# Turning 32 tiles of an expert table by VectorE in an earlier layer instead of by TensorE where they are used

## The chip, the cores and the metric

One core of one Trainium2 chip runs the whole program. The metric is the device time of one execution in microseconds. TensorE (PE) multiplies, VectorE (DVE) and ScalarE (ACT) do elementwise work, GpSimd (POOL) here does almost nothing but issue DMAs, SyncE (SP) issues the DMAs of the weight stream.

## What is computed

256 tokens of width 2048 pass through two blocks in float32. Only two parts matter here. The first is the feed-forward layer of the first block:

```python
def swiglu(h, w_gu, w_down):
    g, u = jnp.split(h @ w_gu, 2, axis=-1)
    return (jax.nn.silu(g) * u) @ w_down
```

with 5632 hidden units. The second is the last layer of the second block, which picks 128 of 16384 experts for each token (8 heads, 16 experts each), after q and the scores have been worked out:

```python
    def token_block(args):
        xb, eb, gb = args
        a = jnp.einsum('td,ted->te', xb, u_tab[eb])
        hidden = gb.astype(xb.dtype) * jax.nn.gelu(a)
        return jnp.einsum('te,ted->td', hidden, v_tab[eb])
```

An expert's number is `ia * 128 + ib`. `u_tab` and `v_tab` have 16384 rows of 2048 floats (8 KB), so that 128 rows with the same `ia` are a tile of 1 MB. A final norm follows. `setup_inputs()` fixes all values.

## The kernel before

**The weight stream.** All dense weights come as 292 tiles of 128x2048 floats through `ring` (4 slots), in halves called units. For each unit ACT writes a rounded leading part into `WH` (`split_hi`, L512 to L515), DVE the rest into `WL` (`split_lo`, L527 and L531), and PE multiplies three combinations of parts (L633). `WH` and `WL` hold 4 units, so ACT may begin a unit when PE has finished the one four before it. The first product of the feed-forward layer (`gu`) has 22 chunks of 8 units, the second (`down`) 44 tiles of 2 units, of which DVE handles the greater part in a loop of 4 rounds with 8 tiles (16 units) each.

**The expert stage** starts near 1820 us. Its order of work is a list written once, `ROW_ORDER`, of 576 entries that every engine walks. An entry is one transfer of 1 MB into one of 12 slots of `rows`. A "u" or "v" entry (256 of each) gathers for each of 128 tokens one row of the table by an indirect DMA from POOL; rows whose `ia` is below `N_DENSE` = 32 are skipped by the bounds check. For those 32 tiles the products are formed densely: a "turned" entry loads a whole tile of `u_tab`, a "dense" entry one of `v_tab`, both by plain DMAs from POOL (L1400). POOL issues entry n when entry n - 12 has been used, strictly in order.

- "u": DVE multiplies the gathered rows with the tokens and sums (L2566).
- "v": in the first part of the list by PE with a diagonal matrix that ACT writes (`DIAG`, L1873; 4 matmuls of 512 columns, L1313); after it mostly by DVE.
- "turned": PE turns the tile in four parts of four 128x128 transposes (`turn_u`, L1249) into a bank, ACT copies each part to `UT` (`keep_turned_u`, L1895), PE multiplies four of them at a time with the turned tokens `HNT` (`u_products`, L1260). Parts 0 and 1 are turned at the entry itself, parts 2 and 3 only in `finish_u`, which PE reaches at the next "v" or "turned" entry; POOL may refill the slot after part 3 has been turned (semaphore `raw_turned`).
- Each pair of tiles then passes through ACT and DVE for its gelu (`square_u`, `poly_u` L2609, `tanh_u`, `gelu_u`).

The 256 "u" entries form 16 groups of 16. `LEADS` says how many "v" entries are mixed into each group (119 in all), `U_TILES` how many "turned" ones (2 in groups 0 to 7, 4 in groups 8 to 11, none after). The other 137 "v" entries and the 32 "dense" ones follow. At the end of each group ACT waits for DVE's polynomial, takes its tanh (L1949), and only then goes on with diagonals. Matmuls in float32 show as two records each, so a "v" entry on PE shows as x8 and a tile's sixteen products as x32.

Of the kernel before, what the change touches and what calls it, by code (L numbers as in the profile page):

```python
# [9 lines left out]
P = 128  # L10
D = 2048
KD = D // P
TOK = 256
# [37 lines left out]
LEADS = [0] + [9] * 7 + [5] * 4 + [9] * 4  # L51
# [43 lines left out]
RAW_TURNED = 24  # L95
_count = {"dve": 0, "pe": 0, "turned": RAW_TURNED}
for _tab, _g, _j in ROW_ORDER:
    _by = "turned" if _tab == "turned" else "pe" if _tab == "dense" or _tab == "v" and by_matmul(PEER_K * _g + _j - N_LEAD) else "dve"
    _count[_by] += 4 if _by == "turned" else 1
    ROW_DONE.append((_by, _count[_by]))  # L100
FINISHED_AT = {}
for _n, (_tab, _g, _j) in enumerate(ROW_ORDER):
    if _tab == "turned":
        FINISHED_AT[_g] = next(n for n in range(_n + 1, ROW_LAST) if ROW_ORDER[n][0] in ("v", "turned"))
SQUARE_AT, POLY_AT, TANH_AT, GELU_AT = ({FINISHED_AT[2 * p + 1] + later: p for p in range(N_DENSE // 2)} for later in (2, 5, 8, 11))
# [9 lines left out]
WEIGH_AT.update({ROW_AT["u", 0, 3 + 2 * g]: g for g in range(EARLY)})  # L115
LAST_DENSE = ROW_AT["dense", N_DENSE - 1, 0]
# [114 lines left out]
def hybrid_block(nc, stream, par, consts, xT, memT, subk, gfin_row, u_tab, v_tab, bias_scratch, bias_rows, out):  # L231
# [5 lines left out]
    with ExitStack() as ctx:  # L237
# [27 lines left out]
        UT0, _ = place("UT0", [P, 4, P], at=at)  # L265
# [59 lines left out]
        AH, AL, _ = split_views("A", a - KD * TOK, 8)  # L325

# [85 lines left out]
        UT = [UT0[:, :, :], PA[:, W_GATE:W_GATE + 4 * P].rearrange("p (k i) -> p k i", i=P)]  # L412
# [5 lines left out]
        IA_GATE = [v.rearrange("p k i -> p (k i)").rearrange("p (k a) -> p k a", a=N_DENSE) for v in UT]  # L418
# [208 lines left out]
        def _(pe):  # L627
# [610 lines left out]
            def turn_u(n, d, part):  # L1238

                q = 4 * d + part  # L1240
                if part == 0:
                    pe.wait_ge(sem(f"row_in{n % ROWS}"), 16 * (n // ROWS + 1))
                if q >= 2:
                    pe.wait_ge(sem("transposes_kept"), TT + q - 1)
                else:
                    pe.wait_ge(sem("norm_leading"), 8 * len(TURNED) + 8)
                for k in range(4):
                    at = (4 * part + k) * P
                    last = nc.tensor.transpose(ps[:, 6 + q % 2, k * P:(k + 1) * P], rows[:, SLOTS[n % ROWS], at:at + P], ident)  # L1249
                last.then_inc(sem("raw_turned"), 1)  # L1250

            def u_products(d, part):

                q = 4 * d + part
                if d % 2 == 0 and part == 0 and d >= 4:
                    pe.wait_ge(sem("gelu_done"), 1 + d // 2 - 1)
                pe.wait_ge(sem("transposes_kept"), TT + q + 1)
                for k in range(4):
                    kt = 4 * part + k
                    last = mm(ps[:, 4 + d // 2 % 2, d % 2 * TOK:(d % 2 + 1) * TOK], UT[q % 2][:, k, :], HNT[kt // 8][:, kt % 8, :],  # L1260
                              start=kt == 0, stop=kt == KD - 1)
                last.then_inc(used, 1)

            def finish_u(n, d):

                u_products(d, 0)
                turn_u(n, d, 2)
                u_products(d, 1)
                turn_u(n, d, 3)
                u_products(d, 2)  # L1270
                u_products(d, 3)

            def turn_ids(tt):

                pe.wait_ge(sem("gates_ready"), 1 + PEER_H * (tt + 1))
                pe.wait_ge(sem("transposes_kept"), TT + 4 * N_DENSE)
# [18 lines left out]
            def dense_rows(n, c):  # L1295
                pe.wait_ge(sem(f"row_in{n % ROWS}"), 16 * (n // ROWS + 1))
# [7 lines left out]
            def gathered_rows(n, g, k):  # L1304
                pe.wait_ge(sem(f"row_in{n % ROWS}"), 16 * (n // ROWS + 1))
# [11 lines left out]
            k, turned = 0, None  # L1317
            for n, (tab, g, j) in enumerate(ROW_ORDER):
# [6 lines left out]
                elif tab == "turned":  # L1325
                    if turned:
                        finish_u(*turned)
                    turn_u(n, g, 0)
                    turn_u(n, g, 1)
                    turned = n, g  # L1330
                elif tab == "v" and (ROW_DONE[n][0] == "pe" or n >= FIRST_SHARED):
                    gathered_rows(n, g, k)
                    k += 1
                    if turned:
                        finish_u(*turned)
                        turned = None
# [3 lines left out]
        def _(pool):  # L1340
# [31 lines left out]
            pool.dma_start(bass.AP(bias_scratch.tensor, 0, [[KD, P], [1, KD]]), PA[:, W_GFFN:W_GFFN + KD]).then_inc(sem("bias_stored"), 16)  # L1372
            pool.wait_ge(sem("down_added"), 8)
# [12 lines left out]
            for n, (tab, g, j) in enumerate(ROW_ORDER):  # L1386
# [8 lines left out]
                elif n >= ROWS:  # L1395
                    by, count = ROW_DONE[n - ROWS]
                    pool.wait_ge(sem({"dve": "rows_dve", "pe": "rows_pe", "turned": "raw_turned"}[by]), count)
                if tab in ("dense", "turned"):
                    table, ia = (v_tab, g) if tab == "dense" else (u_tab, U_ORDER[g])
                    pool.dma_start(rows[:, SLOTS[n % ROWS], :], table[ia * PEER_KEYS:(ia + 1) * PEER_KEYS, :]).then_inc(sem(f"row_in{n % ROWS}"), 16)  # L1400
# [11 lines left out]
        def _(act):  # L1412
# [183 lines left out]
            W.until(T_IN2 - 2)  # L1596
# [1184 lines left out]
```

## Time and profile before

| | |
|---|---|
| median of 3 runs | 3148.67 us (3145.7 to 3165.38) |
| profiled execution | 3147.76 us, span 3146.0 us, mean granted clock 0.972 |
| PE busy | 2904.2 us (92%) |
| DVE busy | 2150.8 us (68%) |
| ACT busy | 1225.1 us (39%) |
| POOL busy | 974.6 us (31%) |
| DMA | 793.69 MB, mean 252 GB/s |

The span runs from the first to the last instruction; the execution's own time is 1.76 us longer. Busy shares are means over stages that differ: in the first 1820 us the weight stream sets the DMA traffic, after it the 1 MB entries of the expert stage. The granted clock is given as a share of full speed.

### The profile page before, as it was taken

How to read it: one execution, taken by the hardware profiler on the slowest of the kernel's cores; microseconds unless marked ns; L12 is line 12 of the kernel's file. 1: busy time of each engine (PE TensorE's matmuls, PEld its weight loads, DVE VectorE, ACT ScalarE, POOL GpSimd, SP SyncE). 2: the span in 40 equal slices, each digit the busy share in tenths (PEclk: the TensorE clock that was granted, in tenths of full speed). 3: DMA queues.
4: the chain of work that ended last, by engine and by line, in shares of the span. 5: the costliest groups of instructions: out<-in, count | busy, mean ns of one | idle time of the engine just before them, and what ended most of it. 6: DMA issues, size and time to landing. Idle time of an engine off the chain costs nothing.

```text
span 3146.0 us, 38089 instructions
## 1 busy us (share of the span) xinstructions
PE 2904.2 (92%) x13724; PEld 2187.2 (70%) x13724; DVE 2150.8 (68%) x2908; ACT 1225.1 (39%) x2125; POOL 974.6 (31%) x599
## 2 busy tenths in 40 slices
PE   9999999999999999999999949888888989978987
PEld 8888788888888889998888945554555655533333
DVE  5686665555565545465565887888887668887777
ACT  5555555555553345355655521111111235700000
POOL 0011000000000000000000056777764678886774
PEclk9999999999999999999999979999998999999998
DMA  7444545555555555543443468999997899999997
GB/s 272 146 165 145 185 182 190 188 187 187 188 185 187 187 187 181 189 157 137 153 177 143 182 262 322 366 380 377 370 365 294 321 338 366 360 389 389 387 405 300
DMA packets 128209, 793.69 MB, mean 252 GB/s; under 512 B 30982, under 2 KB 30998, under 8 KB 32670
## 3 DMA queue, kind: packets, MB, share of 16 engines
q0 software_dynamic: 84000, 475.94, 39.2%
q1 hardware_dynamic: 43920, 313.73, 27.4%
q8 instruction: 90, 1.47, 0.2%
q10 hardware_dynamic: 144, 2.10, 0.2%
q14 instruction: 55, 0.45, 0.0%
HBM read 925.55 MB, written 4.22 MB: 296 GB/s over the span
## 4 chain that ended last, share of the span: by engine, by line
PE 69%; POOL 9%; DVE 8%; DMA 8%; issue 3%; ACT 3%; DVEq 0%; ACTq 0%; SPq 0%; POOLq 0%
PE ps L633 48%; POOL rows L1405 9%; PE ps L1313 6%; PE ps L1260 4%; DMA rows<-peer_v 4%; DMA rows<-peer_v,arena 3%; PE ps L1300 3%; DVE arena L2566 3%; PE ps L1249 1%; PE ps L741 1%; DVE WL L531 1%; ACT arena L1885 0%; PE ps L941 0%; PE ps L1291 0%; DMA rows<-peer_u,arena 0%
## 5 line engine op out<-in xcount | busy, mean ns | idle before, releaser
L531 DVE SCALAR_TENSOR_TENSOR WL<-ring,PA,WH 128x512 fp32r<-128x512 f32 x896 | 633.2, 753 | 459.5 <-ACT WH L515 442.6
L1313 PE MATMUL ps<-rows,rstd 128*128 128x512 f32 x1108 | 531.9, 632 | 158.1 <-ACT rstd L1873 103.4
L2566 DVE CUSTOM_DVE_ANT_0 arena<-rows,arena 128x2048 f32<-128x2048 f32 x256 | 586.9, 2292 | 64.5 <-DMA rows<-peer_u,arena 25.8
L514 ACT ACTIVATE WH<-ring,PA 128x512 fp32r<-128x512 f32 x448 | 324.1, 723 | 545.8 <-PE ps L633 398.4
L1405 POOL DMA_INDIRECT rows<-peer_u,arena x256 | 456.2, 1782 | 213.5 <-DVE WL L531 85.1
L1313 PEld LDWEIGHTS ps<-rows,rstd 128*128 128x128 f32 x1108 | 217.8, 202 | 428.6 <-issue 366.6
L1405 POOL DMA_INDIRECT rows<-peer_v,arena x256 | 447.0, 1746 | 171.5 <-issue 65.5
L633 PE MATMUL ps<-WH,HH 128*128 128x512 f32 x1120 | 442.3, 395 | 4.2 <-DVE WL L531 4.2
L633 PE MATMUL ps<-WH,HL 128*128 128x512 f32 x1120 | 437.7, 391 | 0.0
L633 PE MATMUL ps<-WL,HH 128*128 128x512 f32 x1120 | 437.2, 390 | 0.0
L2570 DVE SCALAR_TENSOR_TENSOR XR<-rows,arena,XR 128x2048 f32<-128x2048 f32 (+1 forms) x119 | 276.7, 2325 | 79.9 <-DMA rows<-peer_v,arena 71.3
L515 ACT ACTIVATE WH<-ring,PA 128x512 fp32r<-128x512 f32 x448 | 317.1, 708 | 0.0
L633 PE MATMUL ps<-HH,WH 128*128 128x256 f32 x1088 | 309.5, 284 | 4.7 <-DVE WL L531 3.2
L633 PE MATMUL ps<-HL,WH 128*128 128x256 f32 x1088 | 307.8, 283 | 0.0
L633 PE MATMUL ps<-HH,WL 128*128 128x256 f32 x1088 | 307.8, 283 | 0.0
L1377 POOL DMA_DIRECT2D arena<-bias_rows x2 | 1.8, 908 | 904.0 <-DVE XR L2275 904.0
L1300 PE MATMUL ps<-rows,arena 128*128 128x512 f32 x512 | 236.8, 618 | 37.7 <-DMA rows<-peer_v 37.7
L527 DVE TENSOR_TENSOR WL<-ring,WH 128x1024 fp32r<-128x1024 f32 x128 | 156.0, 1224 | 164.5 <-ACT WH L512 163.8
L633 PEld LDWEIGHTS ps<-WH,HH 128*128 128x128 f32 x1120 | 211.2, 189 | 49.1 <-DVE WL L531 5.7
L633 PEld LDWEIGHTS ps<-WH,HL 128*128 128x128 f32 x1120 | 210.8, 188 | 44.5
L633 PEld LDWEIGHTS ps<-WL,HH 128*128 128x128 f32 x1120 | 211.3, 189 | 43.1 <-issue 0.5
L1300 PEld LDWEIGHTS ps<-rows,arena 128*128 128x128 f32 x512 | 99.7, 198 | 173.0 <-issue 119.2
(391 smaller groups left out, 4186.6 us busy)
## 6 DMA issues: line engine op xcount, KB each, us to landing
ring<-stream SPq DMA_DIRECT2D x292, 1024.0 KB, 4.8
rows<-peer_u POOLq DMA_DIRECT2D x32, 1024.0 KB
rows<-peer_v POOLq DMA_DIRECT2D x32, 1024.0 KB
rows<-peer_u,arena POOLq DMA_INDIRECT x256
rows<-peer_v,arena POOLq DMA_INDIRECT x256
arena<-xT SPq DMA_DIRECT2D x4, 512.0 KB, 8.8
bias_rows<-bias_scratch POOLq DMA_DIRECT2D x1, 2048.0 KB, 11.4
arena<-xT ACTq DMA_DIRECT2D x1, 2048.0 KB, 10.7
```

What stands on the lines that cost most here:

```text
L514: nc.scalar.activation(half_tile(WH, u)[:, 0:CH], raw_half(u)[:, 0:CH], ACT.Copy, scale=gain[0])
L515: nc.scalar.activation(half_tile(WH, u)[:, CH:UNIT], raw_half(u)[:, CH:UNIT], ACT.Copy, scale=gain[1]).then_inc(hi_done, 1)
L527: nc.vector.tensor_tensor(half_tile(WL, u), raw_half(u), half_tile(WH, u).bitcast(f32), ALU.subtract).then_inc(split, 1)
L531: ins = nc.vector.scalar_tensor_tensor(out=half_tile(WL, u)[:, s], in0=raw_half(u)[:, s], scalar=gain[d], in1=half_tile(WH, u).bitcast(f32 ...
L633: last = mm(o, l, r, start=start and n == 0, stop=stop and n == 2)
L741: last = mm(o, k[:, 2 * h + d, tk * P:(tk + 1) * P], q[:, 2 * h + d, tq * P:(tq + 1) * P], start=d == 0, stop=d == 1)
L1260: last = mm(ps[:, 4 + d // 2 % 2, d % 2 * TOK:(d % 2 + 1) * TOK], UT[q % 2][:, k, :], HNT[kt // 8][:, kt % 8, :], start=kt == 0, stop=kt = ...
L1300: last = mm(ps[:, 4 * tt + q, :], DENSE[c][:, tt * P:(tt + 1) * P], rows[:, SLOTS[n % ROWS], q * CH:(q + 1) * CH], start=False, stop=tt == ...
L1313: last = mm(ps[:, 4 * tt + q, :], DIAG[:, k % DIAGS, :], rows[:, SLOTS[n % ROWS], q * CH:(q + 1) * CH], start=n == mine[0], stop=n == ends[q])
L1405: nc.gpsimd.indirect_dma_start(out=rows[:, SLOTS[n % ROWS], :], out_offset=None, in_=u_tab if tab == "u" else v_tab, in_offset=bass.Indire ...
L2566: ins = V.tensor_tensor_reduce(out=JUNK, in0=rows[:, SLOTS[n % ROWS], :], in1=HN[:, tt, :], scale=1.0, scalar=0.0, op0=ALU.mult, op1=ALU.a ...
L2570: ins = V.scalar_tensor_tensor(out=XN[:, tt, s], in0=rows[:, SLOTS[n % ROWS], s], scalar=GA[:, tt, at:at + 1], in1=XN[:, tt, s], op0=ALU.m ...
```

## The change

The 32 tiles of `u_tab` are turned ahead of time and stored. From the start of the feed-forward layer on, POOL loads each tile as four DMAs of 256 KB (pieces of 2 KB: 32 rows by a quarter of the columns on 32 partitions each) into two half buffers, DVE turns the 32x32 blocks of each half with one instruction (`turn_tile`, 1024 elements per partition), and POOL stores the 1 MB result to a DRAM table `u_turned`, waits until it has landed, and loads the next tile. Twenty tiles are turned in `gu`, one a chunk, after unit 3; the other twelve in `down`, three a round, after units 1, 6 and 11 of 16. The expert stage then loads tiles from `u_turned` and PE multiplies them at once (`turned_rows`); its transposes, ACT's copies and their waits are removed. The columns of the tokens are picked with a step of 16 to match. "v" entries move: groups 8 to 11 get 8 in place of 5, groups 12 to 14 get 8 in place of 9, so that 128 stand in the first part and 128 after it. ACT waits once, ahead of the next norm, until all tiles are stored. The gelu steps of a pair stand 4, 7, 10 and 13 entries after its second tile (before: 2, 5, 8, 11 after the entry that finished it).

```diff
-LEADS = [0] + [9] * 7 + [5] * 4 + [9] * 4
+LEADS = [0] + [9] * 7 + [8] * 7 + [9]
...
+LANDED = [32 * N_DENSE, 32 * N_DENSE, 16 * N_DENSE] + [0] * (ROWS - 3)
...
+        U_TURNED, a = take(a, KD, 4, 32)
+        U_HALF0, _ = take(a, 2, 512)
+        U_HALF = [U_HALF0, rstd[:, :, :].rearrange("p (b x) t -> p b (x t)", b=2)]
+        u_turned = nc.dram_tensor("u_turned", (N_DENSE, P, D), f32, kind="Internal").ap()
...
-                        last = nc.tensor.transpose(ps[:, b, k * TOK + tt * P:k * TOK + (tt + 1) * P], HN[:, tt, (2 * b + k) * P:(2 * b + k + 1) * P], ident)
+                        last = nc.tensor.transpose(ps[:, b, k * TOK + tt * P:k * TOK + (tt + 1) * P], HN[:, tt, 2 * b + k:D:KD], ident)
...
+            def turned_rows(n, d):
+
+                pe.wait_ge(sem(f"row_in{n % ROWS}"), LANDED[n % ROWS] + 16 * (n // ROWS + 1))
+                if d == 0:
                     pe.wait_ge(sem("norm_leading"), 8 * len(TURNED) + 8)
...
+                if d % 2 == 0 and d >= 4:
                     pe.wait_ge(sem("gelu_done"), 1 + d // 2 - 1)
...
+                u = rows[:, SLOTS[n % ROWS], :].rearrange("p (k i) -> p k i", i=P)
+                for k in range(KD):
+                    last = mm(ps[:, 4 + d // 2 % 2, d % 2 * TOK:(d % 2 + 1) * TOK], u[:, k, :], HNT[k // 8][:, k % 8, :],
+                              start=k == 0, stop=k == KD - 1)
+                last.then_inc(sem("rows_pe"), 1)
...
+            pool.wait_ge(sem("small_weights"), 4)
+            for d in range(N_DENSE + 1):
+                if d:
+                    pool.wait_ge(sem("small_weights"), 4 + 2 * d)
+                    pool.dma_start(u_turned[d - 1], U_TURNED.rearrange("p k b i -> p (k b i)")).then_inc(sem("row_in2"), 16)
+                    pool.wait_ge(sem("row_in2"), 16 * d)
+                if d < N_DENSE:
+                    for b in range(4):
+                        at = (U_ORDER[d] * PEER_KEYS + 32 * b) * D
+                        pool.dma_start(U_HALF[b // 2][:, b % 2, :], bass.AP(u_tab.tensor, at, [[512, 4], [D, 32], [1, 512]])).then_inc(sem(f"row_in{b // 2}"), 16)
             pool.wait_ge(sem("down_added"), 8)
...
+                    tile = v_tab[g * PEER_KEYS:(g + 1) * PEER_KEYS, :] if tab == "dense" else u_turned[g]
+                    pool.dma_start(rows[:, SLOTS[n % ROWS], :], tile).then_inc(sem(f"row_in{n % ROWS}"), 16)
...
             W.until(T_IN2 - 2)
+            act.wait_ge(sem("row_in2"), LANDED[2])
...
+            def turn_tile(d, i=0, per=0):
+
+                for h in range(2):
+                    dve.wait_ge(sem(f"row_in{h}"), i * (32 * per) + 32 * (d + 1))
+                    V.transpose(U_TURNED[:, :, 2 * h:2 * h + 2, :],
+                                U_HALF[h].rearrange("p b (d k) -> p k b d", k=KD)).then_inc(sem("small_weights"), 1)
...
                 for m in range(first, 8):
                     split_lo(dve, 2 * (T_GU + 4 * n) + UNITS + m, i)
+                    if 1 <= n < N_GU - 1 and m == 3:
+                        turn_tile(n - 1, i, 2)
...
+                    for m in range(8):
+                        split_lo(dve, 2 * (T_DOWN + 4 * j) + UNITS + m, i)
+                        if (j, m) in ((0, 1), (0, 6), (1, 3)):
+                            turn_tile(N_GU - 2 + 2 * j + m // 6, i, 3)
                     act_batch(j + 2, i)
```

## Rows read from the trace of the kernel before

**Rows 1.** Part 2 of the page, 40 slices: DMA busy share in tenths
```profile
DMA  7444545555555555543443468999997899999997
```

**Rows 2.** Part 4 of the page: the chain that ended last, by line
```profile
PE ps L633 48%; POOL rows L1405 9%; PE ps L1313 6%; PE ps L1260 4%; DMA rows<-peer_v 4%; DMA rows<-peer_v,arena 3%; PE ps L1300 3%; DVE arena L2566 3%; PE ps L1249 1%; PE ps L741 1%; DVE WL L531 1%; ACT arena L1885 0%; PE ps L941 0%; PE ps L1291 0%; DMA rows<-peer_u,arena 0%
```

**Rows 3.** Stretches: busy PE, PEld, DVE, ACT, POOL; granted clock; DMA share; GB/s
```profile
600.00:900.00 300.00, 300.00 (x1352) 248.31 (x1351) 173.31 (x258) 160.22 (x258) 0.00 (x0) 1.00 0.52 189
950.00:1150.00 200.00, 200.00 (x859) 161.15 (x858) 102.93 (x90) 76.27 (x72) 0.00 (x0) 1.00 0.53 189
1850.00:1900.00 50.00, 15.66 (x56) 10.72 (x56) 41.83 (x72) 3.73 (x9) 19.40 (x12) 0.60 0.47 169
1900.00:2300.00 400.00, 350.50 (x1147) 203.74 (x1148) 344.19 (x614) 60.26 (x155) 314.44 (x185) 0.96 0.97 373
2300.00:2750.00 450.00, 390.33 (x1655) 259.95 (x1654) 350.32 (x475) 172.45 (x422) 313.55 (x191) 0.96 0.90 339
2350.00:2450.00 100.00, 78.54 (x324) 55.29 (x323) 71.11 (x131) 18.76 (x41) 50.42 (x37) 0.90 0.76 283
2750.00:3100.00 350.00, 300.23 (x707) 132.03 (x706) 273.49 (x135) 8.90 (x24) 254.64 (x167) 0.95 0.99 392
```

**Rows 4.** Timeline of PE from 2368 us: start, length, line, operation
```profile
2368.84 1.89 PE L1260 MATMUL ps<-arena,UT 128*128 128x256 f32 x8
2370.57 0.60 PE L1249 MATMUL ps<-CO,rows 128*128 128x128 f32 x4
2371.01 1.89 PE L1260 MATMUL ps<-arena,PA 128*128 128x256 f32 x8
...
2376.63 1.04 PE L1249 MATMUL ps<-CO,rows 128*128 128x128 f32 x8
2378.83 3.67 PE L1313 MATMUL ps<-rows,rstd 128*128 128x512 f32 x8 [1.17 <-ACT rstd L1873]
```

**Rows 5.** Timeline of POOL: two issues that waited
```profile
1896.36 0.99 POOL L1405 DMA_INDIRECT rows<-peer_v,arena  x1 [19.46 <-PE ps L1249]
...
2373.64 0.57 POOL L1400 DMA_DIRECT2D rows<-peer_u  x1 [15.73 <-PE ps L1249]
```

**Rows 6.** Waits from 2300 to 2750 us: total, times, longest
```profile
DVE arena L2609 <- ACT arena L1908: 56.4, 9, 8.6
PE ps L1313 <- ACT rstd L1873: 55.9, 24, 7.7
...
POOL rows L1400 <- PE ps L1249: 47.0, 6, 15.7
```

**Rows 7.** Groups by line, 1850 to 3146 us: busy, mean ns, idle before
```profile
L2566 DVE CUSTOM_DVE_ANT_0 arena<-rows,arena 128x2048 f32<-128x2048 f32 x249 | 570.8, 2292 | 63.3 <-DMA rows<-peer_u,arena 25.8 <-DVE arena L2545 3.4 <-DVE arena L2603 3.1
...
L1249 PE MATMUL ps<-CO,rows 128*128 128x128 f32 x496 | 70.3, 275 | 4.0 <-DMA rows<-peer_u 4.0
```

**Rows 8.** VectorE, 950 to 1150 us by form, and line 2297 by itself
```profile
L527 DVE TENSOR_TENSOR WL<-ring,WH 128x1024 fp32r<-128x1024 f32 x72 | 88.2, 1225 | 97.4 <-ACT WH L512 97.4
...
L2252 DVE TENSOR_SCALAR A_h<-arena 128x1024 fp32r x8 | 5.5, 689 | 0.0
...
L2297 DVE TENSOR_TENSOR arena<-arena,PA x8: 566/570/596, 1287.3 to 1290.7; 128x240 f32<-128x240 f32 x8
```

**Rows 9.** Timeline of ACT, `down`: two units, seven apart
```profile
949.87 1.06 ACT L512 ACTIVATE WH<-ring 128x1024 fp32r<-128x1024 f32 x1 [1.74 <-PE ps L633]
...
969.47 1.06 ACT L512 ACTIVATE WH<-ring 128x1024 fp32r<-128x1024 f32 x1 [1.74 <-PE ps L633]
```

**Rows 10.** DMA issues: count, KB each, median us to landing
```profile
ring<-stream SPq DMA_DIRECT2D x292, 1024.0 KB, 4.8
...
arena<-memT POOLq DMA_DIRECT2D x1, 2048.0 KB, 9.0
...
arena<-subkeys POOLq DMA_DIRECT2D x1, 1024.0 KB, 7.7
...
out<-arena SPq DMA_DIRECT2D x1, 1024.0 KB, 3.9
```

More of the change, by code:

```diff
@@ L94 @@
 ROW_DONE = []
-RAW_TURNED = 24
-_count = {"dve": 0, "pe": 0, "turned": RAW_TURNED}
+_count = {"dve": 0, "pe": 0}
 for _tab, _g, _j in ROW_ORDER:
-    _by = "turned" if _tab == "turned" else "pe" if _tab == "dense" or _tab == "v" and by_matmul(PEER_K * _g + _j - N_LEAD) else "dve"
-    _count[_by] += 4 if _by == "turned" else 1
+    _by = "pe" if _tab in ("dense", "turned") or _tab == "v" and by_matmul(PEER_K * _g + _j - N_LEAD) else "dve"
+    _count[_by] += 1
     ROW_DONE.append((_by, _count[_by]))
[L101 to L105, printed above, removed]
+SQUARE_AT, POLY_AT, TANH_AT, GELU_AT = ({ROW_AT["turned", 2 * p + 1, 0] + later: p for p in range(N_DENSE // 2)} for later in (4, 7, 10, 13))
 BATCH_AT = {}
@@ L1315, in gathered_rows @@
                 last.then_inc(sem("rows_pe"), 1)
-            k, turned = 0, None
+            k = 0
             for n, (tab, g, j) in enumerate(ROW_ORDER):
@@ L1325, in _ @@
                 elif tab == "turned":
[L1326 to L1330, printed above, removed]
+                    turned_rows(n, g)
                 elif tab == "v" and (ROW_DONE[n][0] == "pe" or n >= FIRST_SHARED):
@@ L1881, in one_hots @@
                 else:
-                    act.wait_ge(used, 2 * N_TILES + 4 * N_DENSE)
+                    act.wait_ge(sem("rows_pe"), ROW_DONE[ROW_AT["turned", N_DENSE - 1, 0]][1])
                 v = ONE_HOT[n % 2]
@@ L1901, in square_u @@
             def square_u(p):
-                act.wait_ge(used, 2 * N_TILES + 8 * p + 8)
+                act.wait_ge(sem("rows_pe"), ROW_DONE[ROW_AT["turned", 2 * p + 1, 0]][1])
                 if U_ORDER[2 * p] // 8 in (2, 3):
@@ L1920, in _ @@
             DIAG_READ = [ROW_DONE[n][1] for n, row in enumerate(ROW_ORDER) if row[0] == "v" and ROW_DONE[n][0] == "pe"]
-            k, turned = 0, None
+            k = 0
             for g in range(EARLY):
@@ L1932, in _ @@
                     tanh_u(TANH_AT[n])
-                if tab == "turned":
-                    if turned is not None:
-                        keep_turned_u(turned, 2)
-                        keep_turned_u(turned, 3)
-                    keep_turned_u(g, 0)
-                    keep_turned_u(g, 1)
-                    turned = g
                 if tab == "v" and (ROW_DONE[n][0] == "pe" or n >= FIRST_SHARED):
@@ L1942, in _ @@
                     k += 1
-                    if turned is not None:
-                        keep_turned_u(turned, 2)
-                        keep_turned_u(turned, 3)
-                        turned = None
                 if tab == "u" and j == PEER_K - 1:
```

56 lines of the change are left out of this document (6 added, 50 removed).

## The prediction, made before the changed kernel was run

> **What bounds the kernel now.** I read the slices first: DMA is about half busy for the first 23 slices and nearly full after that, with a dip near slice 30 [rows 1]. The chain that ended last puts 48% of the span on L633, the matmuls of the weight stream; the rest is a mix of POOL's issues, DMA landings, PE and DVE [rows 2]. So there are two programs in a row, and the stretches price them. In the feed-forward layer PE is busy all the time at full clock while DVE has 173.31 of 300 us of work and the DMA engines are 0.52 busy: PE is the bound, and DVE, POOL and DMA have room [rows 3]. In the expert stage the DMA engines are 0.97 busy from 1900 to 2300 us and 0.99 from 2750 to 3100 us, at 373 and 392 GB/s: there DMA is the bound, though PE has 350.5 of 400 us and DVE 344.2. Two stretches fall out: 1850 to 1900 us (share 0.47) and 2300 to 2750 us (0.90, and 0.76 in its worst 100 us) [rows 3]. What the change can win lies in these two holes; it does not touch the bytes that the stage moves. Rows of POOL name the reason for both: it stood 19.46 us in the first and 15.73 us in the second until PE had turned a tile (L1249), because entries are issued in order and a "turned" slot comes free only after its last transposes [rows 5].
>
> **What leaves PE.** On PE's timeline a step of eight product records takes 1.73 us (2368.84 to 2370.57) and a group of four transposes 0.44 us (to 2371.01) [rows 4]. A tile has four of each: 6.9 + 1.8 = 8.7 us, and 6.9 us after the change. 32 x 1.8 = 56 us of PE leave. None of that is gain where DMA bounds; it counts through the holes. ACT's copies go too, and with them the 1.17 us by which a "v" entry waited for a diagonal queued behind a copy [rows 4], part of 55.9 us of such waits from 2300 to 2750 us [rows 6]. The 7.7 us ones among them stay possible: ACT still waits for DVE at a group's end.
>
> *First hole.* The slot of the second tile now comes free when its products are done and no longer waits for the first "v" entry, which itself waits for ACT and DVE. Up to 19 us of issue come forward. But DVE is busy 41.8 of these 50 us, the same share as later (344.2 of 400), and at most 12 entries can be held ahead, so not all is kept: between 0 and -19 us, I take -12.
>
> *1900 to 2300 us.* DMA share 0.97; smaller waits on PE go. 0 to -8 us (to the 0.99 of the later stretch, 400 x 0.02), I take -4.
>
> *Second hole.* At a share of 0.97 the same transfers take 450 x 0.90 / 0.97 = 417.5 us, -32.5; by the rate 450 x 339 / 373 = 409 us, -41. I take -34, nearer the share, as a byte costs the same in both. What is late next is PE: a group of groups 8 to 11 now holds 4 tiles (27.7 us) and 8 "v" entries of about 3.5 us (28.1), 55.8 us. Its DMA work: 24 gathered entries of which a quarter of the rows is skipped (32 of 128 `ia`), and 4 whole ones, 22 MB of 1.049e6 bytes each at 373 GB/s, 61.9 us. PE would be 0.90 busy. From 1900 to 2300 us it was 0.88 busy beside a DMA share of 0.97, so it nearly fits; for the last 2% and engines waiting in order I add 5 us. From 0 to -41, taken -29.
>
> *Moved "v" entries.* Nine of the tail's 137 come forward, 9 x 0.75 x 1.049 = 7.1 MB, moved at 373 instead of 392 GB/s: +1 us. Eight DVE steps of 2.29 us [rows 7] in the tail become PE steps of 3.5 us, both beside a full DMA.
>
> *Tokens with a step of 16.* 32 transposes of 0.11 us each on an otherwise waiting path, at most doubled: 0 to 3.5 us, I take +1. Loads from the new table have the same 8 KB rows: nothing.
>
> **What is added in the feed-forward layer.** The trace has no block transpose. Contiguous two-input work costs 1225 ns for 1024 elements and 2292 ns for 2048 [rows 7, 8], so 1.04 ns an element and 0.16 us fixed. The nearest row is L2297, which also reads every 16th element: 570 ns for 240, so 1.71 ns an element [rows 8]. For 1024: T = 1.9 us. Bounds: 0.69 us (L2252, one input) and 2.45 us (twice L527). I take 1.9, as the access is the same; a pair costs 3.8 us, 32 pairs 122 us of DVE. In `gu` a chunk takes 22.2 us (100 PE records of the 1352 in 300 us), DVE is busy 12.8 us of it. The pair delays what is queued behind it on DVE, units 4 and on, for which PE waits. Its cover is the lead of three units (8.3 us) less ACT's and DVE's work on one, (173.31 + 160.22)/300 x 2.77 = 3.1 us: 5.2 us, more than 3.8. Cost nothing; without the cover up to 20 x 3.8 = 76 us.
>
> The Trainium skill, page "SBUF — State Buffer", section "Specifications (TRN2)", says that an access needs at least two hits in a 16-byte line for full bandwidth. By it a read with a step of 64 bytes is slow; the row of L2297 agrees, and with full speed instead (1.2 us each) nothing in the sum would change.
>
> The chain tile by tile is store, landing, four loads, landing, transposes; DVE waits for the loads with the stream's units behind it, and PE behind those. Landing of the store: between 3.9 us (1 MB out, alone on SP's queue) and 7.7 us (`subkeys`, POOL), I take 5.5. Loads: between 4.8 us (`ring`, 1 MB) and 9.0 us (`memT`, 2 MB), I take 6.5, as four issues follow each other [rows 10]. Transposes that are not hidden: when DVE waits, the first half is turned while the second lands, 2.8 us. Handing over 0.3 us. C = 15.1 us; from 9.7 us (3.9 + 4.8 + 0.7 + 0.3) to 22 us (7.7 + 9.0 + 4.9 + 0.3). In `gu` there are 22.2 us for it: hidden. In `down` a unit takes 19.6 / 7 = 2.80 us [rows 9], and from the first of the twelve tiles to the last are 58 units, 162.4 us, for 11 C; DVE's lead there is 3 x 2.80 - 1.06 - 1.23 = 6.1 us [rows 8, 9]. So the stall is 11 C - 168.5 where that is positive: 11 x 15.1 = 166, nothing, but the threshold of C = 15.3 is close. I take +2. ACT's new wait comes after the last store by more than four tiles of the stream: nothing. SP's ring loads share the engines: 2.1 MB more in 14.9 us is 141 GB/s, by the 0.53 for 189 GB/s a share of 0.92 in all [rows 3]; with four slots of 5.6 us ahead they have cover. POOL's next queued work, the bias loads, waits for the layer's end anyway.
>
> Against the four small loads stands the Trainium skill, page "DMA: Bandwidth & Descriptors", section "Bandwidth": batch to 1 MiB or more; it gives 6.15 us for a 1 MB load from GpSimd. As an estimate from that page, two such transfers make C 15.4 us and the stall 1 us; no row here shows a 256 KB piece.
>
> **Sum.** -12 - 4 - 29 + 1 + 1 + 2 = -41 us against the profiled execution's 3147.76 us: 3107 us. That execution lies 0.9 us under the median of 3148.67 us, which is the figure to compare with.
>
> **Rivals.**
> *The chain doesn't fit `down`.* One mechanism: C above 15.3 us, while DVE holds back the stream. For it: loads, stores and stream share engines at 0.92, and a landing under load may be far above the 4.8 us of a half-busy stretch; against it, 2 MB landed in 9.0 us. At C = 20: 51.5 us of stall, -43 + 51.5, so 3156 us. It is slower than before from C = 19.2 on. Chance 0.13.
> *PE or the coupling of engines stays the bound in groups 8 to 11.* In the worst 100 us PE was only 0.79 busy though it was the one waited for [rows 3]. DVE's 56.4 us for ACT's squares and the group-end waits speak for it [rows 6]; that these waits came from late transposes (POOL's 47.0 us) against. At 0.79 a group takes 55.8 / 0.79 = 70.6 us, 35 us more in four groups than DMA needs; the second hole stays open: -12 + 1 + 1 + 2, 3140 us. Chance 0.17.
> *DMA runs everywhere as in the tail.* -19 - 8 - 41 + 1, 3081 us. For it the rate of 392 GB/s; against it PE's and DVE's loads of near 0.9. Chance 0.13.
> The forecast, 3090 to 3125 us, has 0.57.
>
> **Range and chances.** 3082 to 3152 us: it leaves out half of the third rival and most of the first. Within 1% (31.5 us, about what a measurement of this kernel can tell from no change) lie a fifth of the forecast's cases, the second rival and most of the first: 0.37. Faster by more (under 3117 us): 0.58. Slower by more needs C above 22 us: 0.05.
>
> **What would show it.** In `gu`: PE busy throughout, transposes of about 1.9 us. In `down`: twelve tiles 14 to 17 us apart and PE still full; waits of DVE on U's loads with PE behind them would be the first rival. At 1850 to 1900 us a DMA share near 0.7 and no wait of POOL near 19 us. From 2300 on a share of 0.95 or more, groups 8 to 11 about 62 us each, L1895 gone; many waits of POOL for L1260's successor there would be the second rival. The tail shorter by 18 us. I would be wrong most likely through C, which rests on landings under a load that the trace doesn't show.

## The result, and the profile after

The changed kernel takes 3209.98 us (median of 4 runs, 3200.68 to 3217.28) against 3149.43 us for the kernel before (median of 4): ratio 1.0185, interval 1.0146 to 1.0225. It is 61 us slower; the forecast was 41 us faster, with a range of 3082 to 3152 us. The profiled execution took 3217.28 us, with a span of 3215.5 us.

The slices of the page show where. These three are the granted clock, the DMA share and the count of packets of the changed kernel:

```profile
PEclk9999999999999888999999998989999999999999
DMA  7344558999997786544444447999999999999997
...
DMA packets 167628, 860.93 MB, mean 268 GB/s; under 512 B 58118, under 2 KB 58134, under 8 KB 67998
```

Against [rows 1] two things changed. The dip near slice 30 is gone: the expert stage is full from end to end. And ten slices of the feed-forward layer, half busy before, now stand at six to nine tenths, while the clock dips at their end: PE stood there for part of the time. The chain that ended last says nothing of the layer: its shares add up to 60%, and the list in order of time begins at 1311 us, behind the layer. So its 14% for the stream's products must not be set against the 48% of [rows 2].

```profile
PE 29%; POOL 10%; DVE 8%; DMA 8%; issue 3%; ACT 2%; DVEq 0%; ACTq 0%; POOLq 0%
PE ps L632 14%; POOL rows L1384 10%; PE ps L1289 6%; DVE arena L2538 3%; DMA rows<-peer_v 3%; PE ps L1276 3%; PE ps L1246 3%; DMA rows<-peer_u,arena 2%; DMA rows<-peer_v,arena 2%; PE ps L940 0%; DVE WL L530 0%; PE ps L996 0%; PE ps L1267 0%; ACT arena L1865 0%; DVE arena L223 0%
```

Lengths of the stages, each between the starts or ends of fixed instructions (VectorE's last work on the small weights just ahead of `gu`, the first split of the layer's activations, the first addition of `down`'s sums, the first "u" entry, a group's last tanh, the last sum). They are worked out from the traces, in microseconds:

| kernel | `gu` | `down` | to the first "u" | 16 groups | tail |
|---|---|---|---|---|---|
| before | 456.3 | 259.1 | 648.2 | 949.1 | 365.0 |
| after | 483.3 | 350.6 | 649.4 | 917.0 | 344.9 |
| change | +27.0 | +91.5 | +1.2 | -32.1 | -20.1 |

So the stage that the change is made for gained 52 us, more than the 43 us of the sum, and the layer that was to hide the turning lost 118.5 us. The changes add up to 67.5 us, and with 2.0 us ahead of the layer to the 69.5 us between the two profiled executions. The medians are 61 us apart, as the profiled execution was the slowest of the four.

Two stretches of the layer, of the changed kernel (columns as in [rows 3]):

```profile
600.00:900.00 300.00, 291.31 (x1296) 238.69 (x1295) 211.40 (x273) 153.67 (x246) 42.74 (x65) 0.99 0.94 271
950.00:1150.00 200.00, 154.89 (x614) 121.87 (x613) 99.91 (x83) 56.43 (x57) 26.31 (x40) 0.90 0.76 215
```

PE issued 1296 records in 300 us of `gu` in place of 1352, and 614 in 200 us of `down` in place of 859. In `down` it is busy for 154.89 of 200 us. The stream and the turning together moved only 215 GB/s there, so the bytes are not what fills the time.

What everyone waited for in `down`, from 925 to 1260 us (total, times, longest):

```profile
POOL u_turned L1346 <- DVE arena L2183: 222.8, 13, 33.0
ACT WH L511 <- PE ps L632: 218.8, 75, 14.4
DVE arena L2183 <- DMA arena<-peer_u: 108.7, 12, 13.9
PEld ps L632 <- DVE WL L526: 72.8, 12, 11.0
PE ps L632 <- DVE WL L526: 67.6, 11, 10.6
POOL arena L1351 <- DMA u_turned<-arena: 52.0, 12, 4.7
```

Read from the third row: DVE waited 108.7 us for the tiles' loads, about once a tile; PE waited behind it for DVE's part of the stream (67.6 us, 11 times); ACT waited behind PE. One link of it, on POOL's timeline (start, length, line, operation, idle before):

```profile
999.29 0.58 POOL L1346 DMA_DIRECT2D u_turned<-arena  x1 [13.36 <-DVE arena L2183]
1004.48 1.37 POOL L1351 DMA_DIRECT2D arena<-peer_u  x2 [4.61 <-DMA u_turned<-arena]
1005.84 1.35 POOL L1351 DMA_DIRECT2D rstd<-peer_u  x2
1024.34 0.58 POOL L1346 DMA_DIRECT2D u_turned<-arena  x1 [17.15 <-DVE arena L2183]
```

and on DVE's:

```profile
1004.16 2.36 DVE L526 TENSOR_TENSOR WL<-ring,WH 128x1024 fp32r<-128x1024 f32 x2
1020.38 1.89 DVE L2183 STREAM_TRANSPOSE arena<-arena 128x1024 f32<-128x1024 f32 x1 [13.86 <-DMA arena<-peer_u]
1022.20 1.85 DVE L2183 STREAM_TRANSPOSE arena<-rstd 128x1024 f32<-128x1024 f32 x1
1023.97 4.59 DVE L526 TENSOR_TENSOR WL<-ring,WH 128x1024 fp32r<-128x1024 f32 x4
```

This round of the chain took 25.05 us: 5.2 us from the store's issue to the first load's, 15.9 us until DVE had the first half, 3.7 us of transposes, 0.3 us to the next store. DVE stood for 13.86 us of it; once released it did four units in a row, the ones that PE was waiting for. The twelve stores of the tiles turned in `down`, from 978.45 to 1232.77 us, are 23.1 us apart on average, and the twenty of `gu`, from 486.23 to 937.66 us, 23.8 us. C is not 15.1 us. On average over eleven rounds of `down` the four parts were 4.9, 13.6, 4.3 and 0.3 us, and DVE stood waiting for the loads in all eleven, so that the chain and not the stream set these intervals. (The expectations below speak of 23.5 and, for eight loads, of 19.6 us: these are means over fewer of the tiles. From here on C is the mean of the eleven intervals of the last twelve stores.)

The DMA issues (count, KB each, median us to landing) name the part that is long:

```profile
u_turned<-arena POOLq DMA_DIRECT2D x32, 1024.0 KB, 4.4
...
arena<-peer_u POOLq DMA_DIRECT2D x64, 256.0 KB, 8.3
rstd<-peer_u POOLq DMA_DIRECT2D x64, 256.0 KB, 12.7
```

The store lands in 4.4 us. The loads of the first half take 8.3 us and those of the second 12.7 us, where a load of 1 MB of `ring`, issued by SP, takes 5.1 us. A DMA of a quarter of the size takes about twice as long.

### The profile page after: what moved, and what is told of

The parts are those of the page before. It is cut to its first block, busy times and chain, and to the rows that moved or that the text cites. A ratio compares the mean times of both kernels' runs of the same rounds, so it can differ in the third digit from the quotient of the medians.

```text
span 3215.5 us, 37171 instructions
## 1 busy us (share of the span) xinstructions
PE 2907.2 (90%) x13276; PEld 2165.1 (67%) x13276; DVE 2243.8 (70%) x2964; ACT 1159.6 (36%) x2005; POOL 1104.7 (34%) x759
## 2 busy tenths in 40 slices
DMA packets 167628, 860.93 MB, mean 268 GB/s; under 512 B 58118, under 2 KB 58134, under 8 KB 67998
## 4 chain that ended last, share of the span: by engine, by line
PE 29%; POOL 10%; DVE 8%; DMA 8%; issue 3%; ACT 2%; DVEq 0%; ACTq 0%; POOLq 0%
PE ps L632 14%; POOL rows L1384 10%; PE ps L1289 6%; DVE arena L2538 3%; DMA rows<-peer_v 3%; PE ps L1276 3%; PE ps L1246 3%; DMA rows<-peer_u,arena 2%; DMA rows<-peer_v,arena 2%; PE ps L940 0%; DVE WL L530 0%; PE ps L996 0%; PE ps L1267 0%; ACT arena L1865 0%; DVE arena L223 0%
## 5 line engine op out<-in xcount | busy, mean ns | idle before, releaser
L1289 PE MATMUL ps<-rows,rstd 128*128 128x512 f32 x1172 | 560.6, 631 | 147.7 <-ACT rstd L1853 90.6
L1289 PEld LDWEIGHTS ps<-rows,rstd 128*128 128x128 f32 x1172 | 231.3, 202 | 443.9 <-issue 359.5
L1384 POOL DMA_INDIRECT rows<-peer_v,arena x256 | 471.1, 1840 | 125.9 <-issue 67.0
L2542 DVE SCALAR_TENSOR_TENSOR XR<-rows,arena,XR 128x2048 f32<-128x2048 f32 (+1 forms) x111 | 257.9, 2324 | 77.6 <-DMA rows<-peer_v,arena 69.7
L1246 PE MATMUL ps<-arena,rows 128*128 128x256 f32 x1024 | 228.0, 381 | 7.7 <-DMA rows<-u_turned 6.6
L511 ACT ACTIVATE WH<-ring 128x1024 fp32r<-128x1024 f32 x128 | 134.6, 1058 | 265.8 <-PE ps L632 258.8
L1246 PEld LDWEIGHTS ps<-arena,rows 128*128 128x128 f32 x1024 | 195.5, 191 | 48.1 <-issue 15.9
## 6 DMA issues: line engine op xcount, KB each, us to landing
rstd<-peer_u POOLq DMA_DIRECT2D x64, 256.0 KB, 12.7
rows<-peer_v,arena POOLq DMA_INDIRECT x256, 13.6
```

Source lines behind the costliest of these rows:

```text
L511: nc.scalar.activation(half_tile(WH, u), raw_half(u), ACT.Copy).then_inc(hi_done, 1)
L1289: last = mm(ps[:, 4 * tt + q, :], DIAG[:, k % DIAGS, :], rows[:, SLOTS[n % ROWS], q * CH:(q + 1) * CH], start=n == mine[0], stop=n == ends[q])
L1384: nc.gpsimd.indirect_dma_start(out=rows[:, SLOTS[n % ROWS], :], out_offset=None, in_=u_tab if tab == "u" else v_tab, in_offset=bass.Indire ...
L2542: ins = V.scalar_tensor_tensor(out=XN[:, tt, s], in0=rows[:, SLOTS[n % ROWS], s], scalar=GA[:, tt, at:at + 1], in1=XN[:, tt, s], op0=ALU.m ...
```

## The experiments

The kernel before took 3152.5, 3153.66 and 3153.28 us on the chips of the three sets of runs below; ratios are against it.

### The two halves of the change, each alone

The stage without the turning (e1):

```diff
-            for d in range(N_DENSE + 1):
-                ... (stores and loads of POOL)
-                        turn_tile(n - 1, i, 2)
-                            turn_tile(N_GU - 2 + 2 * j + m // 6, i, 3)
-                    tile = ... else u_turned[g]
+                    tile = ... else u_tab[U_ORDER[g] * PEER_KEYS:(U_ORDER[g] + 1) * PEER_KEYS, :]
```

> The changed kernel without its work in the feed-forward layer: no loads, transposes or stores there; the expert stage loads the unturned tiles of the table from u_tab in their place (same shape, same bytes; the values of these 32 tiles' products are wrong). If the two parts add up, the expert stage keeps what the two traces show: its first u row to its last sum took 3136.9 - 1822.8 = 1314.1 us before and 3206.4 - 1944.5 = 1261.9 us after, 52 us less, so 3149 - 52 = 3097 us. A rival: part of the 52 us comes from elsewhere (the table in internal DRAM, the state in which the stage begins); then the time is above 3110 us.

Measured: 3102.85 us, ratio 0.9841 (0.981 to 0.9872). `gu` 456.3, `down` 260.6, groups 918.3, tail 347.4 us. The time lies between the 3097 us expected and the 3110 us of the rival.

The turning without the stage (e2, the kernel before, with POOL's loop and `turn_tile`, and its own expert stage):

```diff
+            for d in range(N_DENSE + 1):
+                ... (stores and loads of POOL, as in the change)
+                        turn_tile(n - 1, i, 2)
+                            turn_tile(N_GU - 2 + 2 * j + m // 6, i, 3)
```

> The kernel before, with the changed kernel's loads, block transposes and stores added in the feed-forward layer and their result not used. If the loss lies only in that layer and does not depend on the new expert stage: 3148 + 121 = 3269 us, with the twelve tiles of the second product about 24 us apart. If the loss came from something else that changed with the stage, it stays well under 3240 us.

Measured: 3264.95 us in one run. `gu` 484.2, `down` 353.3, groups 944.9, tail 361.7 us; the last twelve stores are 23.4 us apart. It is 4 us from the 3269 us expected.

The halves add up: the stage alone gains some 50 us, the turning alone costs about 112 us, together about the 60 us lost. The whole loss is made in the layer, and the gain in the stage does not depend on it. Removing the stores and loads together with the transposes does not yet say which of them costs.

### Which property of the loads is slow

The four loads of a tile read pieces of 2 KB with the pattern `[[512, 4], [D, 32], [1, 512]]`: the outermost dimension is the 4 strips of columns. The next kernels keep the number of loads and their bytes and change the pattern alone, or the size of the piece.

Rows outermost, 128 of them (e3):

```diff
-  at = (U_ORDER[d] * PEER_KEYS + 32 * b) * D
-  bass.AP(u_tab.tensor, at, [[512, 4], [D, 32], [1, 512]])
+  at = U_ORDER[d] * PEER_KEYS * D + 512 * b
+  bass.AP(u_tab.tensor, at, [[D, 128], [1, 512]])
```

> The changed kernel with each of the four loads of a tile taking a piece of 2 KB from each of 128 rows of the tile, one row for each partition, in place of four strips of 32 rows (same bytes, same size of piece, same number of DMAs; the columns land in other places, so the 32 tiles' products are wrong). Theory A, the order of the strips (slowest dimension of 4) makes the loads slow: they land in 7 us or less instead of 8 to 13, the tiles of the second product come 15 to 18 us apart and the time falls by 60 us or more, to 3150 us or less. Theory B, pieces of 2 KB are slow by themselves, or the weight stream's bursts hold the loads back: no change, 3200 to 3217 us.

Measured: 3124.18 us in one run; `gu` 456.4, `down` 285.2 us; 17.2 us a tile. Theory A holds. The trace of this run gives no landings; from a tile's first load to DVE's first transpose passed 7.0 us on average in `down`, in place of 13.6.

Two loads of 512 KB, 4 KB a row (e4):

```diff
+  bass.AP(u_tab.tensor, at, [[D, 128], [512, 2], [1, 512]])     # two of these in place of four
```

> The changed kernel with two loads of 512 KB for a tile, 4 KB from each row, one row for each partition (same bytes; the 32 tiles' products are wrong). If the size of the piece or the number of DMAs is what makes the loads slow, they land in about 6 us, the chain falls to 16 to 18 us and the time to 3120 to 3150 us, while the kernel with 2 KB from each row stays slow. If the weight stream's bursts hold any load back, it stays within 20 us of the changed kernel, 3195 us or more.

Measured: 3106.84 us in one run; `gu` 456.3, `down` 267.9 us; 15.8 us a tile. It is 13 us below the expected range, and as e3 was not slow, the size of the piece or the number of DMAs is not what makes the changed kernel's loads slow.

With the same bytes in the same number of loads as the changed kernel, the rows-outermost form takes 5.9 us less a tile, and `gu` loses nothing. But it differs in two ways: the 4 is gone, and a load takes 2 KB of each of 128 rows in place of the whole of 32. So the outermost dimension was changed by itself, with the rows-outermost form as the base:

```diff
+  [[D, 4], [4 * D, 32], [1, 512]]       # e6
+  [[D, 16], [16 * D, 8], [1, 512]]      # e7
```

> As the kernel with one row for each partition (3124 us), with the same 128 pieces of 2 KB in each load, but dealt to the partitions by a pattern that counts 4 outermost: partition 32c + r takes row c + 4r. The 32 tiles' products are wrong. Theory A1, the slowest dimension of 4 is what makes the loads slow (few DMA engines share the work): back to 3195 to 3217 us, small packets back to some 58 thousand. Theory A2, it was the addresses (four neighbouring pieces of one row in four strips): stays at 3115 to 3135 us.

> The same with 16 outermost: partition 8c + r takes row c + 16r. The 32 tiles' products are wrong. By theory A1 16 is enough for all engines: 3115 to 3135 us. If any pattern that is not a plain run of rows is slow: 3195 us or more.

Measured, one run each: 3231.01 us with 4 outermost (`gu` 496.8, `down` 350.8 us, 23.2 us a tile) and 3135.51 us with 16 (`gu` 456.4, `down` 292.5 us, 18.1 us a tile). The first is 14 us above the range of theory A1 and the second at its upper end. The page's count of packets, first of the kernel with 4 outermost, then of that with 16:

```profile
DMA packets 167628, 860.93 MB, mean 267 GB/s; under 512 B 58118, under 2 KB 58134, under 8 KB 67998
```

```profile
DMA packets 143053, 860.73 MB, mean 275 GB/s; under 512 B 33543, under 2 KB 33559, under 8 KB 43423
```

and their stretch from 950 to 1150 us, in the same order:

```profile
950.00:1150.00 200.00, 160.37 (x635) 126.62 (x633) 104.76 (x93) 60.36 (x65) 26.39 (x40) 0.90 0.78 216
```

```profile
950.00:1150.00 200.00, 178.36 (x716) 140.84 (x714) 123.19 (x95) 63.74 (x61) 29.59 (x56) 0.94 0.79 268
```

Both read rows, 2 KB of each, into 128 partitions, four loads a tile. The one with 4 outermost is the changed kernel over again: the same 58118 small packets, 216 GB/s at a DMA share of 0.78, 95.5 us apart in the whole from the one with 16. At the same share the 16 moved 268 GB/s. The outermost dimension is the property. (With it the row that a partition takes changes too, c + 4r or c + 16r; no run holds that fixed, but e3, with neither order, is as fast as the one with 16 to within 11 us.) The count of small packets is a fingerprint of it. The kernel before has 30982. The difference over 32 tiles is 848 a tile for the changed kernel, 80 for the rows-outermost form and 48 for its form with two loads: 16 small packets for each DMA of these (5 and 3 of them with the store), and (848 - 16) / 4 = 208 for each load with 4 outermost.

The Trainium skill, page "DMA: Bandwidth & Descriptors", section "Why a DMA increments its semaphore by 16 and not by 1", says that the number of engines of a DMA is the largest up to 16 that divides the slowest dimension of both patterns, so 4 for these loads and 16 for the others. The runs agree in effect: 4 is slow, 16, 32 and 128 are not.

The packet records in the traces tell the two paths by which the 4 could cost time (few engines, or the extra small packets) apart. A load of 256 KB is 64 packets of 4 KB in both kernels. With 4 outermost 192 packets of 8 bytes come on top (24576 in all; the kernel before and the one with 16 have none). They took 11 ns each, 8.8 us a tile in all, half a microsecond if spread over 16 engines, against 5.0 us a tile between the two kernels: their own time is not the path. With 4 outermost, 4 or 8 of the 4 KB packets were in flight at once for 9 and 12% of the time in which any was (3, 5, 7 and 9 for 3 to 6% each); with 16 outermost 4 and 8 have 5 and 3%, and 16 at once has 24% in place of 10%. That is what four engines to a load would give. The records do not name the engine, so it is argued and not shown. A 4 KB packet also took longer, 351 ns in place of 233; why stays open.

### The tiles of the change, without the 4

Each load goes to the 32 partitions of one strip, so that rows can be outermost; eight loads of 128 KB, everything is computed (e5):

```diff
-  for b in range(4):
-      at = (U_ORDER[d] * PEER_KEYS + 32 * b) * D
-      pool.dma_start(U_HALF[b // 2][:, b % 2, :], bass.AP(u_tab.tensor, at, [[512, 4], [D, 32], [1, 512]]))
+  for h in range(2):
+      for c in range(4):
+          at = (U_ORDER[d] * PEER_KEYS + 64 * h) * D + 512 * c
+          pool.dma_start(U_HALF[h][32 * c:32 * c + 32, :, :], bass.AP(u_tab.tensor, at, [[D, 32], [32 * D, 2], [1, 512]]))
```

> The changed kernel with eight loads of 128 KB for a tile, one for each strip of 32 partitions and half (32 outermost), the same bytes in the same places as in the changed kernel, the whole computed. By theory A1 the transfers are fast again, but POOL issues eight times 0.68 us in place of four, 2.7 us more for each tile: 3124 us of the run with plain rows plus up to 11 x 2.7, so 3125 to 3155 us. By A2 it stays above 3190 us.

Measured: 3152.03 us, ratio 0.9995 (0.9979 to 1.0012), in the range by A1. `gu` 456.3 us: its loss is gone. `down` 308.8 us, 19.5 us a tile: still 49.7 us too long.

Next (e8), the wait of POOL for the store's landing, 4.1 to 4.7 us of each round, was taken off the loads (POOL issues the next loads at once; only DVE waits for the store, before it writes the buffer again):

```diff
                     pool.dma_start(u_turned[d - 1], ...)
-                    pool.wait_ge(sem("row_in2"), 16 * d)
                 ... (the eight loads)
+                if d:
+                    pool.wait_ge(sem("row_in2"), 16 * d)
+                    pool.sem_inc(sem("u_stored"), 1)
```

> The kernel with eight loads, in which POOL no longer waits for the store's landing before it issues the next loads; DVE waits for it ahead of the next transposes (a semaphore that POOL raises after the landing). The whole computed. Some 4.8 us leave the chain of each tile; if the chain is what holds back the second product, all of it goes: 3100 to 3112 us, as with the expert stage alone (3103 us). If it is DMA traffic as such, it stays within 10 us of the run with eight loads.

Measured: 3147.47 us, ratio 0.998 (0.9963 to 0.9996); `down` 302.5 us. That is 4.6 us below the eight loads, with intervals that overlap: the second outcome and not the first, which is missed by 35 us. POOL's timeline shows what came in place of the wait:

```profile
1002.12 0.59 POOL L1347 DMA_DIRECT2D u_turned<-arena  x1 [14.47 <-DVE arena L2188]
1002.71 2.12 POOL L1352 DMA_DIRECT2D arena<-peer_u  x4
1004.82 2.12 POOL L1352 DMA_DIRECT2D rstd<-peer_u  x4
1020.95 0.59 POOL L1347 DMA_DIRECT2D u_turned<-arena  x1 [14.01 <-DVE arena L2188]
```

The loads start 0.6 us after the store instead of 5, and the round still takes 18.8 us (18.9 us on average, 19.5 us with the wait). Beside the store and the stream the loads take that much longer: from the first load's issue to the end of the transposes 18.1 us on average in `down`, in place of 14.3. Of the 4.4 us of the wait, 0.6 us were to be had.

### Time for the chain instead of a shorter chain

In `down` the tiles stand 5, 5 and 6 units apart (14 to 17 us). The chain of 19.5 us does not fit; 8 units, 22.4 us, would. The layer has room: tile 21 into `gu`, two tiles a round in `down`, and three in the units after the loop (e9).

```diff
-                    if 1 <= n < N_GU - 1 and m == 3:
+                    if 1 <= n and m == 3:
                         turn_tile(n - 1, i, 2)
...
-                        if (j, m) in ((0, 1), (0, 6), (1, 3)):
-                            turn_tile(N_GU - 2 + 2 * j + m // 6, i, 3)
+                        if m == 3:
+                            turn_tile(N_GU - 1 + j, i, 2)
...
+            W.units_to(2 * (T_DOWN + 32) + UNITS + 4)
+            turn_tile(N_DENSE - 3)
             ... (the last two tiles after units + 12 and + 19)
```

> The eight loads of e5 (each to 32 partitions), and the 32 tiles spread evenly over the layer: one in each of 21 chunks of `gu`, two a round of `down` (8 units apart), three in the units that follow the loop of `down`; everything is computed. Tiles then stand 8 units, 22.2 to 22.4 us apart, where e5 took 19.6 us from store to store. If what `down` loses is only 11 C against the 162 us of its 58 units (the period of the stream against that of the chain), there is no stall left: `gu` 456, `down` 260 to 263, the stages after as in e1, so 3102 to 3112 us, a ratio of 0.984 to 0.987. Rival 1: the turning costs `down` by its presence (the engines and DVE shared with the stream, whose unit 3 of cover is shorter in `down`), by the tile: eleven tiles at 4.5 us each (49.7 / 11 in e5) would be about 3152 again. Rival 2: part of each, 3120 to 3140 us.

Measured: 3107.22 us, ratio 0.9859 (0.984 to 0.9879), in the expected range. `gu` 456.4, `down` 261.0, to the first "u" 649.8, groups 917.6, tail 344.5 us. The two stretches of this kernel:

```profile
600.00:900.00 300.00, 300.00 (x1352) 248.27 (x1351) 219.16 (x284) 160.47 (x257) 66.69 (x125) 1.00 0.88 283
950.00:1150.00 200.00, 200.00 (x859) 161.12 (x857) 135.77 (x108) 75.36 (x71) 45.78 (x81) 1.00 0.87 279
```

PE is busy throughout with the same 1352 and 859 records as in [rows 3]; the turning takes place beside it, at a DMA share of 0.87. DVE's timeline shows the cover at work:

```profile
1017.12 1.23 DVE L526 TENSOR_TENSOR WL<-ring,WH 128x1024 fp32r<-128x1024 f32 x1 [1.57 <-ACT WH L511]
1018.27 1.97 DVE L2184 STREAM_TRANSPOSE arena<-arena 128x1024 f32<-128x1024 f32 x1
1020.16 1.92 DVE L2184 STREAM_TRANSPOSE arena<-rstd 128x1024 f32<-128x1024 f32 x1
1022.00 2.32 DVE L526 TENSOR_TENSOR WL<-ring,WH 128x1024 fp32r<-128x1024 f32 x2
```

No idle time ahead of a transpose: the tile was there, and one unit was late and done in a pair. The rival, a price by the tile, falls: `down` loses 49.7 us with its tiles planned at 14 to 17 us and 1.9 us with them at 22.4 us.

The same kernel with the old list of entries (e10, `LEADS = [0] + [9] * 7 + [5] * 4 + [9] * 4`):

> e9 with the list of entries of the kernel before (groups 8 to 11 hold 5 `v` entries in place of 8, groups 12 to 14 nine in place of eight). If the gain of the expert stage comes from the work that leaves PE, it stays: the stage as long as in e9 within 5 us, with more entries in the tail and fewer in the groups. If it comes from filling the hole of groups 8 to 11 with more entries, groups 8 to 11 stay short of transfers and the whole is 10 to 25 us slower than e9.

Measured: 3101.97 us, ratio 0.9842 (0.9813 to 0.9872), which overlaps with that of the list of the change. Groups together 898.5 us, tail 364.8 us: 1263.3 us in all, against 1262.1 us. Groups 8 to 11 take 214.0 us with 25 entries each, 239.2 us with 28, and 251.6 us with 25 in the kernel before. So the hole is closed by the work that left PE, and the moved entries are worth nothing either way: 25 us of transfers go from one place to another. The 10 to 25 us that the second theory gave to them did not come.

And with the four loads of the changed kernel, at the even spacing (e11):

```diff
     for b in range(4):
         ... bass.AP(u_tab.tensor, at, [[512, 4], [D, 32], [1, 512]])
```

> The four loads of the changed kernel (outermost dimension of 4) with e9's even spacing. The chain took 23.5 us a tile against 22.2 to 22.4 us between tiles. By the period alone: `gu` keeps its loss of 27 us, `down` loses 1.2 x 10 to 2 x 10 = 12 to 20 us in place of 91, so 3140 to 3155 us. If the placement in `down` mattered little and the landing itself grows with what is free, `down` loses 50 us or more: above 3180 us.

Measured: 3164.63 us in one run. `gu` 489.9, `down` 289.7, to the first "u" 654.9 us; ten stores from 964.64 to 1184.95 us are 24.5 us apart. It is 10 us above the expected range, as `gu` lost 33.6 us in place of 27 (21 tiles for 20) and the stretch to the first "u" 6.7 us. The order of size holds: with more time between tiles `down` loses 30.6 in place of 91.5 us, but a chain longer than 22.4 us fits nowhere in the layer. Both repairs are needed.

## Why the prediction was wrong

*Where the gain lies: right for the holes.* The hole near 1900 us was to gain 12 us and the stretch after it 4; groups 1 to 7, from the first group's last tanh to the eighth's, went from 418.4 to 403.1 us, 15.3 us less. For the second hole the sum took 34 us less 5. With the old list, where the entries are the same, groups 8 to 11 gained 37.6 us. Three stretches of the spread kernel (e9):

```profile
1850.00:1900.00 50.00, 17.57 (x48) 11.00 (x49) 46.40 (x79) 3.43 (x10) 30.77 (x18) 0.66 0.82 299
1900.00:2300.00 400.00, 338.27 (x946) 186.11 (x945) 348.15 (x621) 32.80 (x99) 312.86 (x183) 0.93 0.96 367
2300.00:2750.00 450.00, 404.18 (x1544) 255.95 (x1543) 370.57 (x498) 140.06 (x368) 357.98 (x209) 0.95 0.96 371
```

In the first hole the share rose from 0.47 to 0.82, more than the 0.7 forecast, and POOL's longest wait there fell from 19.46 to 8.7 us; as an estimate from these rates, (299 - 169) x 50 / 373 = 17 us of transfers. The stretch after it did not move towards 0.99: 0.96 and 367 GB/s, where it had 0.97 and 373. So the 4 us taken for it did not come, and that the sum of the two terms fits to 1 us is in part luck.

In the second hole a share of 0.96 in place of 0.90 [rows 3], "0.95 or more" as forecast; a group of groups 8 to 11 takes 59.8 us, where 61.9 us of transfers were worked out. The second rival did not come true: PE still waited 37.5 us for late diagonals from 2300 to 2750 us (55.9 before), but the transfers kept their pace. Tail and groups together gained 52 us for 43.

*The price of a transpose: right.* Taken 1.9 us by the row of L2297 [rows 8] and not 1.2; the row of the changed kernel:

```profile
L2183 DVE STREAM_TRANSPOSE arena<-arena x32: 1891/1969/1994, 482.1 to 1226.7; 128x1024 f32<-128x1024 f32 x32
```

*Its cover in `gu`: right.* The lead of three units hides the pair: with loads that come in time (eight loads, e5 and e9) `gu` takes 456.3 and 456.4 us.

*The landing of a tile's loads: the step that failed.* The sum took 6.5 us "between 4.8 us (`ring`, 1 MB) and 9.0 us (`memT`, 2 MB)" and got C = 15.1 us, at most 22. The trace has 12.7 us for the second half, 15.9 us from the first issue until DVE had its data in the round shown, and C = 23.1 us in `down`. That is outside both bounds. Term by term, on average in `down`: the store 4.9 us for 5.5, the loads 13.6 us for 6.5, the transposes 4.3 us for 2.8, handing over 0.3 us as taken. So 7.1 of the 8.0 us are the loads; of the transposes nothing was hidden, as DVE was still short of the second half in only 2 of 11 rounds when it had turned the first. The bounds came from rows of other sizes, and the new loads differ in their pattern: 4 outermost. Nothing in the trace before shows such a load (it has none of the 8-byte packets), so no row of it could have bounded it from above; that this was unknown belonged in the range, where C above 22 us had a chance of 0.05. With 16, 32 or 128 outermost the chain takes 15.8 to 19.5 us. The estimate from the Trainium skill, page "DMA: Bandwidth & Descriptors", section "Bandwidth", was C = 15.4 us for two transfers of 1 MB; the nearest form run here, two loads of half that size and a store, took 15.8 us. The rule on the number of engines, cited above from the same page, spoke against the pattern and was not weighed.

*The rule for the stall: right, with one caution.* The prediction had "11 C - 168.5 where that is positive", and the first rival was priced by it. `down` against the 259.1 us of before:

| kernel | C, us a tile | 11 C - 168.5 | measured |
|---|---|---|---|
| e4, two loads | 15.8 | 5 | 8.8 |
| e3, rows outermost | 17.2 | 21 | 26.1 |
| e7, 16 outermost | 18.1 | 31 | 33.4 |
| e8, no wait for the store | 18.9 | 39 | 43.4 |
| e5, eight loads | 19.5 | 46 | 49.7 |
| after | 23.1 | 86 | 91.5 |
| e6, 4 outermost | 23.2 | 87 | 91.7 |

It holds to within 2 to 6 us over the whole range, whatever made C what it was. The caution: C is measured here between the stores of the same `down`, and a longer `down` would spread these stores whatever held it up, so the agreement by itself is in good part bookkeeping. That the chain was the cause is shown by other things: DVE stood waiting for the loads in 10 or 11 of the 11 rounds of every kernel in the table, and with the same eight loads and 22.4 us between tiles (e9) it never waited and the stall was gone.

So the first rival came true, beyond the C of 20 us that it was priced at, and with a second part that the sum had at nothing: the "22.2 us for it" in `gu` did not hold either, 20 tiles 23.76 us apart where e9 has them 22.24 us apart, 19 x 1.52 = 29 us by that and 27.0 us measured. In all 118.5 us in place of 2. The threshold of 15.3 us was seen and called close, yet even e4's chain, close to the value forecast, lost 8.8 us: the placing in `down` left no room for an error in C.

*The rest.* Tokens picked with a step of 16 and what lies between the layers: +1.2 us, taken +1. The moved entries: taken +1, nothing measurable.

## What to carry to other kernels

Work hidden beside a stream has to fit by its period, not only by its busy time: work out store, landing, issue, load and compute as a chain, and space the pieces by more than that, with a margin for landings under load. Here 22.4 us for a chain of 19.5 turned a draw (0.9995) into 0.9859, though nothing became faster. Before such a load is priced by its bytes, look at its outermost dimension, and price a repair of the order of work (where the pieces stand) ahead of a repair of the chain (a wait taken away).

## What the runs showed of the hardware

- Loads of 256 KB from POOL with an outermost dimension of 4 landed in 8.3 and 12.7 us (median) where a 1 MB load of the stream, from SP, took 5.1 us, and each brought 208 packets under 512 bytes in place of 16. In two kernels that differ in this order alone 4 or 16 outermost gave 3231.01 or 3135.51 us, one run each.
- The extra packets are of 8 bytes, 192 to a load, and took 11 ns each; the 4 KB packets beside them took 351 ns with 4 outermost and 233 ns with 16.
- At a DMA share of 0.78 and 0.79 the engines moved 216 and 268 GB/s with these two patterns: the share does not fix the rate.
- A load issued beside a 1 MB store instead of 5 us later hardly ended earlier: 18.9 and 19.5 us a round.
- With rows outermost a tile took 17.2 us in four loads with 2 KB a row and 15.8 us in two with 4 KB; size of piece and number of loads were not separated.
- A block transpose of 128x1024 float32 that reads every 16th element took 1.97 us (median of 32).
